# A two-layer SwiGLU and mixer trunk on eight cores: later due dates in two listings, joined sums, an end by halves

## The chip, the cores and the metric

One Trainium2 chip, eight cores. Every core runs the same program on one of the eight sequences of the batch (2048 tokens, 1024 channels), so nothing is exchanged between cores. The metric is the device time of the slowest core, in microseconds (us). Engines: TensorE (PE; PEld is its weight load), VectorE (DVE), ScalarE (ACT), GpSimd (POOL), SyncE (SP), and 16 DMA engines per core.

## The reference

Two layers, each three sub-layers; every one is x += gate * f(RMSNorm(x) * (1 + scale) + shift), with gate, scale and shift from the conditioning vector.

```python
for l in range(2):
    mod = silu(c) @ w_mod[l] + b_mod[l]                    # 9 x 1024 values for the sequence
    h, gate = modulate(x, norm_g[l, 0], mod_f1)
    x = x + 0.5 * gate * swiglu(h, w_ffn_in[l, 0], w_ffn_out[l, 0])   # 1024 -> 2 x 2816 -> 1024
    h, gate = modulate(x, norm_g[l, 1], mod_mx)
    if l == 0: y = mixer_ab(h, ...)      # projections to 2560, layernorm + chunk mixing of "v", short conv, projection
    else:      y = mixer_pool(h, ...)    # trailing-window means (2, 4, 8, 16), 256 x 256 per group
    x = x + gate * y
    h, gate = modulate(x, norm_g[l, 2], mod_f2)
    x = x + 0.5 * gate * swiglu(h, w_ffn_in[l, 1], w_ffn_out[l, 1])
return rmsnorm(x, final_g)
```

## The kernel before

**Tiling.** Channels lie on the partitions, tokens in tiles of 512 columns (`TT`). X holds the whole stream in f32 (4 token tiles x 8 chunks of 128 channels). A phase is one sub-layer for one pair of token tiles (p = 0: tiles 0 and 1, p = 1: tiles 2 and 3), ten phases in all; the pooling mixer runs in the background of phases of the second layer.

**Seven products for eight.** A pair of token tiles, a pair of halves of the contraction and a pair of output blocks form a 2 x 2 block product, computed with seven block products instead of eight (`class Unit`, P1 to P7). That needs sums of blocks ahead of TensorE, in f16 on VectorE: of the weights in `piece_sums` (a piece of 128 x 2048 lands in a slot; four dependent 128x512 operations make four more blocks), of h in `h_sums`, of the activations g*u in `a_sums`, called when a gate-up unit is done. There are also sums on the results: P6 and P7 each have a `tensor_tensor` on PSUM (rows `ps<-ps,TP` and `TP<-ps,TP`), and ScalarE copies two PSUM banks per unit. An FFN phase has two groups (m = 5 and 6 blocks per half); each group is gate-up units (28 matmuls each), then four down units (7 m matmuls each), u = 0 to 3, each for two output chunks. `LastUnit` does the same in eight plain products, without sums; before it is used in two groups (`PLAIN`) and for the last down unit of the program.

**Order.** Python code calls `add` for every instruction; `Timeline` gives each a planned start. TensorE's order is that in which the code calls the products: `segments` interleaves unit v's rest with unit u's start (u1 u5 v7 v3 u2 v4 u6, and v4 before u2 where a down unit u follows a gate-up unit v). At the end `relist` (once) sets VectorE's and ScalarE's order anew: of what is ready, the instruction with the earliest due date goes first. A due date is the smaller of what the users of the result need and the planned start plus 8 (`due.append`). `emit` writes one in-order queue per engine, with semaphore waits; all instructions have the line of `op.fn(E)` in `run`, L442 in the profile.

**Mixer of layer 0** (`ab_phase`): per 128 tokens a projection, Gelu, `bn_stats`, `bn_aggr`, two small POOL operations for 1/sqrt, and a `tensor_scalar` on VectorE for the normalised values; then four down units opened as u1 u5 w1 w5 u2 u6 ....

**Statistics.** `squares` makes x^2 on ScalarE and adds pairs on VectorE; `ones_mm` sums over partitions on TensorE. The code puts that matmul into TensorE's order 0.3 after the planned end of the sum, or at once where `bg_drain` empties the background work ahead of a group's down units.

**The end** (`end_phase`): down units 0, 1, 2 in seven products, unit 3 plain: its two chunks for tile 2, then its two for tile 3. Then squares, ones matmul, `rstd` (Ln, Exp on ScalarE), and `final_chunk` for 16 blocks of 128x512: x * g * rstd in one VectorE operation each, and a DMA out per two chunks.

## Time and profile before

| | |
|---|---|
| runs | 1965.75, 1962.3, 1962.87 us; median 1962.87 |
| the profiled execution | 1963.22 us; span of its slowest core 1961.7 us, of all cores 1947.1 to 1961.7 |
| PE / PEld / DVE / ACT / POOL busy | 96% / 44% / 89% / 52% / 9% of the span |
| mean granted TensorE clock | 0.979 to 0.993, by core |

The profiled execution is 1.5 us longer than its span and 0.35 us longer than the median. A matmul's record is longer than its pitch, since matmuls overlap: counts and waits tell more than busy time. "[x <-DVE ...]" behind a row is the time its engine sat idle before it, and who ended that.

### The profile page before, as it was taken

Reading aid. Unit: us, or ns where it says so; the run is one execution under the profiler, and the core shown is the slowest. Engines: PE = TensorE matmul, PEld = TensorE weight load, DVE = VectorE, ACT = ScalarE, POOL = GpSimd, SP = SyncE. Lnnn points to the kernel's source line nnn. Section 1 sums busy time; section 2 is a strip of 40 time slices with the busy share of each in tenths; the row PEclk is TensorE's granted clock in tenths of the full one; section 3 lists DMA queues with packets and bytes.
Section 4 is the critical chain, followed back from the end, with each engine's and each line's share of the span. In section 5 each row is a group of like instructions: output and inputs, shape, how many; then the busy total and the mean of one; then the engine's idle time right before and its main releaser. Section 6 shows DMA issues by size and latency. Waiting matters only on the chain.

```text
span 1961.7 us, 25716 instructions; the slowest of 8 cores (1947.1 to 1961.7 us)
## 1 busy us (share of the span) xinstructions
PE 1883.8 (96%) x8656; PEld 854.2 (44%) x8656; DVE 1749.7 (89%) x3788; ACT 1011.1 (52%) x1692; POOL 172.5 (9%) x330
## 2 busy tenths in 40 slices
PE   6999999999999899999999999999999999899996
PEld 5444444444434344444444444444443444344442
DVE  3989999989998999999999988986999779998985
ACT  4545565455363564465446544655457535664343
...
GB/s 285 163 193 193 157 100 166 167 95 173 192 108 160 107 122 161 182 111 148 153 180 118 129 81 93 83 91 96 75 76 65 97 75 81 59 96 89 165 85 104
DMA packets 67519, 248.73 MB, mean 127 GB/s; under 512 B 7616, under 2 KB 7744, under 8 KB 67136
## 3 DMA queue, kind: packets, MB, share of 16 engines
...
q14 instruction: 54, 0.44, 0.1%
...
## 4 chain that ended last, share of the span: by engine, by line
PE 79%; DVE 11%; DMA 9%; issue 1%; SPq 0%; ACT 0%; POOL 0%; DVEq 0%; POOLq 0%; ACTq 0%
PE ps L442 79%; DVE TP L442 3%; DMA SLOTS<-wout 2%; DMA SLOTS<-win 2%; DVE ACTB L442 2%; DMA ACTB<-wmod 2%; DVE X L442 2%; DVE SLOTS L442 1%; DMA SLOTS<-wab 1%; DVE WMOD L442 1%; DVE ps L442 1%; DMA WMOD<-wmod 1%; DVE SQ L442 1%; SPq L442 0%; DVE H L442 0%
## 5 line engine op out<-in xcount | busy, mean ns | idle before, releaser
L442 PE MATMUL ps<-H,SLOTS 128*128 128x512 f16 x5440 | 1200.3, 379 | 10.4 <-DVE ps L442 4.4
L442 PEld LDWEIGHTS ps<-H,SLOTS 128*128 128x128 f16 x5440 | 530.3, 98 | 659.2 <-issue 29.6
L442 ACT ACTIVATE ps<-ps 128x512 f32<-128x512 f32 x654 | 379.9, 582 | 522.9 <-PE ps L442 490.6
L442 PE MATMUL ps<-ACTB,SLOTS 128*128 128x512 f16 x2716 | 612.6, 382 | 22.1 <-DVE ACTB L442 9.6
L442 DVE TENSOR_TENSOR SLOTS<-SLOTS 128x512 f16<-128x512 f16 x1044 | 415.3, 417 | 27.2 <-DMA SLOTS<-win 14.0
L442 PEld LDWEIGHTS ps<-ACTB,SLOTS 128*128 128x128 f16 x2716 | 263.6, 98 | 358.6 <-issue 55.0
L442 ACT ACTIVATE TP<-ps 128x512 f32<-128x512 f32 x463 | 275.8, 596 | 166.5 <-PE ps L442 164.0
L442 DVE TENSOR_TENSOR ACTB<-TP,ps 128x512 f16<-128x512 f32 x368 | 249.3, 683 | 31.0 <-PE ps L442 18.2
L442 DVE TENSOR_TENSOR TP<-ps,TP 128x512 f32<-128x512 f32 x239 | 164.3, 687 | 68.8 <-ACT ps L442 67.4
L442 ACT ACTIVATE SQ<-X 128x512 bf16<-128x512 f32 x224 | 133.9, 623 | 144.8 <-DVE X L442 102.0
L442 DVE SCALAR_TENSOR_TENSOR X<-ps,GH,X 128x512 f32<-128x512 f32 x257 | 189.5, 745 | 16.2 <-PE ps L442 15.1
L442 POOL DMA_DIRECT2D SLOTS<-win x176 | 93.1, 529 | 1036.5 <-PE ps L442 981.3
L442 DVE SCALAR_TENSOR_TENSOR WMOD<-WMOD,CB 128x512 f32<-128x512 f32 (+1 forms) x258 | 175.7, 688 | 5.6 <-DMA WMOD<-wmod 5.5
L442 DVE TENSOR_TENSOR ps<-ps,TP 128x512 f32<-128x512 f32 x239 | 166.2, 695 | 15.6 <-PE ps L442 11.6
L442 ACT ACTIVATE H<-TP,MODT,AS 128x512 f16<-128x512 f32 x160 | 123.2, 805 | 33.6 <-DVE TP L442 20.2
L442 DVE TENSOR_TENSOR ACTB<-ACTB 128x512 f16<-128x512 f16 x338 | 136.5, 419 | 0.9
L442 DVE TENSOR_TENSOR TP<-X,RS 128x512 f32<-128x512 f32 x192 | 127.5, 683 | 1.2 <-ACT RS L442 0.9
L442 POOL DMA_DIRECT2D SLOTS<-wout x88 | 46.5, 528 | 541.3 <-PE ps L442 541.3
L442 DVE TENSOR_TENSOR SQ<-SQ 128x1024 bf16<-128x1024 bf16 (+1 forms) x104 | 55.6, 541 | 2.3 <-ACT SQ L442 2.2
L442 PE MATMUL ps<-SQ,ONES 128*128 128x512 bf16 x82 | 32.4, 449 | 21.2 <-DVE SQ L442 12.0
L442 DVE SCALAR_TENSOR_TENSOR X<-TP,GH,X 128x512 f32<-128x512 f32 x63 | 46.8, 742 | 0.0
L442 DVE TENSOR_TENSOR H<-H 128x1024 f16<-128x1024 f16 (+1 forms) x72 | 43.4, 623 | 0.1
...
## 6 DMA issues: line engine op xcount, KB each, us to landing
...
ACTB<-wmod SPq DMA_DIRECT2D x10, 512.0 KB, 24.7
...
```

The source lines that it names most:

```text
L442: return lambda E: getattr(E, name)(*a, **k)
```

## The change

- `relist` runs twice, and the planned start plus 40 takes the place of plus 8.
- Joined sums: in `piece_sums` two of four operations become one with a 128x2x512 output, whose first input is a block read twice; the blocks are stored in another order for it (`W11` ... `S4`). `h_sums` and `a_sums` get `two_sums` in the same way, and `a_sums` for m > 4 handles two blocks at a time where it can.
- FFN down units open with two units in step (`run_down`, `ORDER_DOWN`); the other order strings say what the code did before.
- The end: one down unit in seven products (was three), units 1, 2 and 3 plain; all of tile 2 first, then tile 3 in two halves of 256 tokens. The gain g is multiplied in on ScalarE, 1/rms on VectorE for two chunks at once, and stored per half.
- The mixer's normalised values: `activation` on ScalarE with two more small POOL operations for its bias, instead of `tensor_scalar` on VectorE. In the pooling mixer the copy of one column (`SLAST`) goes to ScalarE (24 copies become 18).
- The ones matmul is placed 2.5 (was 0.3) after the sum's planned end.

```diff
+SLACK_DUE = 40.0
-            due.append(o.start + (0.0 if o.eng == "pe" else 8.0))
+            due.append(o.start + (0.0 if o.eng == "pe" else SLACK_DUE))
...
+    W11, W12, W22, W21, S1, S2, S4 = 2, 3, 1, 4, 0, 5, 6
...
-                if (l, i, p, g) not in PLAIN and not (last and g == len(GROUPS) - 1 and 4 * x >= 3 * m):
+                if (l, i, p, g) not in PLAIN and not (last and g == len(GROUPS) - 1 and 4 * x >= m):
...
-        tt_(v(4), v(3), v(2), ALU.add, [k(2), k(3)], [k(4)], n=w, half=True)
-        tt_(v(3), v(0), v(3), ALU.subtract, [k(0), k(3)], [k(3)], n=w, half=True)
-        tt_(v(5), v(4), v(0), ALU.subtract, [k(4), k(0)], [k(5)], n=w, half=True)
-        tt_(v(6), v(1), v(5), ALU.subtract, [k(1), k(5)], [k(6)], n=w, half=True)
+        both = SL[:, s, :].rearrange("p (q k) -> p q k", k=512)
+        add("dve", I("tensor_tensor", out=both[:, S1:W21 + 1:W21 - S1, 0:w], in0=v(W21).unsqueeze(1).broadcast_to([128, 2, w]),
+                     in1=both[:, W22:W11 + 1:W11 - W22, 0:w], op=ALU.subtract), reads=[k(W22), k(W11), k(W21)],
+            writes=[k(S1), k(W21)], cost=c_dve(2 * w, True))
+        tt_(v(S2), v(W11), v(S1), ALU.subtract, [k(W11), k(S1)], [k(S2)], n=w, half=True)
+        tt_(v(S4), v(W12), v(S2), ALU.subtract, [k(W12), k(S2)], [k(S4)], n=w, half=True)
...
-        return [q] if h == 2 else list(range(q, q + h)), op.end + 0.3
+        return [q] if h == 2 else list(range(q, q + h)), op.end + 2.5
...
+    def two_sums(view, at, n, k):
+
+        add("dve", I("tensor_tensor", out=view[:, 1:6:4, at:at + n], in0=view[:, 3, at:at + n].unsqueeze(1).broadcast_to([128, 2, n]),
+                     in1=view[:, 1:5:3, at:at + n], op=ALU.add), reads=k(1) + k(3) + k(4), writes=k(1) + k(5), cost=c_dve(2 * n, True))
...
     def a_sums(m, i, half, apart=False):
         w = 1
+        if not apart and m > 4 and i < m - 2 + m % 2:
+            if i % 2 == 0:
+                return
+            w = 2
+        i += 1 - w
...
+    ORDER_DOWN = "u1 u5 v7 v3 v4 w1 u2 u6 w5 w2 u7 u3 w6 u4"
+    ORDER_AB = "u1 u5 w1 w5 u2 u6 u7 u3 w2 u4 w6"
...
-            ts(Av4[:, blk, :], TP[:, gv, 0:TT], STAT[:, st, 6:7], STAT[:, st, 9:10], ALU.subtract, ALU.mult,
-               [("TP", gv), ("ST", st)], [("A", blk)], n=TT)
+            add("pool", I("tensor_tensor", out=STAT[:, st, 8:9], in0=STAT[:, st, 6:7], in1=STAT[:, st, 9:10], op=ALU.mult),
+                reads=[("ST", st)], writes=[("ST", st)], cost=0.3)
+            add("pool", I("tensor_scalar", out=STAT[:, st, 7:8], in0=STAT[:, st, 8:9], scalar1=-1.0, scalar2=None, op0=ALU.mult),
+                reads=[("ST", st)], writes=[("ST", st)], cost=0.3)
+            act(Av4[:, blk, :], TP[:, gv, 0:TT], AF.Identity, [("TP", gv), ("ST", st)], [("A", blk)], src="sb",
+                scale=STAT[:, st, 9:10], bias=STAT[:, st, 7:8])
...
-                        add("dve", I("tensor_copy", SLAST[:, ch:ch + 1], PMS[:, (tt + 1) * TT - 1:(tt + 1) * TT]), reads=[("PMS", tt)],
-                            writes=[("SLAST", ch)], cost=0.07)
+                        if p == 0 or tt == 0:
+                            act(SLAST[:, ch:ch + 1], PMS[:, (tt + 1) * TT - 1:(tt + 1) * TT], AF.Copy, [("PMS", tt)], [("SLAST", ch)], n=1,
+                                src="sb")
...
+    def run_down(units, side):
+
+        v = pend.pop()
+        a, b = units[:2]
+        for n, f in enumerate(in_order(ORDER_DOWN, u=a, w=b, v=v)):
+            f()
...
+        def scaled(t, c, rk, keys, base=(), lo=0, w=TT):
+
+            out = X[:, t, c:c + 2, lo:lo + w]
+            ok = ("OUT", t, c + 1) if w == TT else ("OUT", t, c + 1, lo)
+            add("dve", I("tensor_tensor", out=out, in0=out, in1=RS[:, t % 2, lo:lo + w].unsqueeze(1).broadcast_to([128, 2, w]), op=ALU.mult),
+                reads=keys + list(base) + rk, writes=keys, cost=c_dve(2 * w))
...
+        pair(0, 0, TT)
+        for lo in (0, W):
+            for u in units:
+                for dd in range(2):
+                    b = bank(hold=True)
+                    u.part(dd, 1, 0, n, b, lo, W)
+                    held.discard(b)
+                    if (u, dd, lo) == (a, 1, 0):
+                        tile2()
+                    flush_halves()
...
-                    run_units([DownUnit(l, s, p, os_, m, u, final) for u in range(3 if final else 4)], side)
+                    units = [DownUnit(l, s, p, os_, m, u, final) for u in range(1 if final else 4)]
+                    (run_units if final else run_down)(units, side)
...
-    Sd.relist()
+    for _ in range(2):
+        Sd.relist()
```

**What the change moves.** TensorE, the opening of the first group of down units in the program, before (banks are numbered; `H,SLOTS` are gate-up products of unit v, `ACTB,SLOTS` down products, five matmuls each):

```order
L442 MATMUL ps5<-ACTB,SLOTS 128x512 x5
L442 MATMUL ps4<-ACTB,SLOTS 128x512 x5
L442 MATMUL ps0<-H,SLOTS 128x512 x4
L442 MATMUL ps1<-H,SLOTS 128x512 x4
L442 MATMUL ps2<-H,SLOTS 128x512 x4
L442 MATMUL ps5<-ACTB,SLOTS 128x512 x5
L442 MATMUL ps3<-ACTB,SLOTS 128x512 x5
L442 MATMUL ps0<-ACTB,SLOTS 128x512 x5
L442 MATMUL ps2<-ACTB,SLOTS 128x512 x5
L442 MATMUL ps3<-ACTB,SLOTS 128x512 x5
```

And with the change:

```order
L445 MATMUL ps4<-ACTB,SLOTS 128x512 x5
L445 MATMUL ps5<-ACTB,SLOTS 128x512 x5
L445 MATMUL ps0<-H,SLOTS 128x512 x4
L445 MATMUL ps1<-H,SLOTS 128x512 x4
L445 MATMUL ps2<-H,SLOTS 128x512 x4
L445 MATMUL ps5<-ACTB,SLOTS 128x512 x5
L445 MATMUL ps4<-ACTB,SLOTS 128x512 x5
L445 MATMUL ps3<-ACTB,SLOTS 128x512 x5
L445 MATMUL ps2<-ACTB,SLOTS 128x512 x5
L445 MATMUL ps5<-ACTB,SLOTS 128x512 x5
```

Before, u2 (the second product into ps5) follows v4 (ps2) at once. With the change, w1 (ps5, now the other unit's bank) stands between v4 and u2 (ps4).

VectorE at the end of the layer-0 mixer, p = 1, between two `ps<-ps,TP` sums that release P3 of the first and of the second down unit (`TP<-X,RS` and `H<-H` build the next phase's h), before:

```order
L442 SCALAR_TENSOR_TENSOR X<-ps,GH,X 128x512
L442 TENSOR_TENSOR TP<-X,RS 128x512 x2
L442 SCALAR_TENSOR_TENSOR X<-ps,GH,X 128x512
L442 TENSOR_TENSOR TP<-X,RS 128x512 x2
L442 TENSOR_TENSOR SLOTS<-SLOTS 128x512
L442 TENSOR_TENSOR H<-H 128x1024
L442 TENSOR_TENSOR SLOTS<-SLOTS 128x512
L442 SCALAR_TENSOR_TENSOR X<-TP,GH,X 128x512
L442 TENSOR_TENSOR H<-H 128x1024 x2
L442 TENSOR_TENSOR ps<-ps,TP 128x512
```

And with the change, from the first of those sums to the second:

```order
L445 TENSOR_TENSOR ps<-ps,TP 128x512
L445 TENSOR_TENSOR TP<-X,RS 128x512 x2
L445 TENSOR_TENSOR SLOTS<-SLOTS 128x2x512
L445 TENSOR_TENSOR TP<-X,RS 128x512
L445 TENSOR_TENSOR TP<-ps,TP 128x512
L445 SCALAR_TENSOR_TENSOR X<-ps,GH,X 128x512 x3
L445 TENSOR_TENSOR ps<-ps,TP 128x512
```

Before, 19 instructions lie between the two sums, sums of h among them (the last part is shown); with the change 8 do, none of them on H.

The last instructions of VectorE, before:

```order
L442 SCALAR_TENSOR_TENSOR X<-ps,GH,X 128x512
L442 TENSOR_TENSOR SQ<-SQ 128x512
L442 SCALAR_TENSOR_TENSOR X<-ps,GH,X 128x512 x2
L442 SCALAR_TENSOR_TENSOR X<-X,SM,RS 128x512 x2
L442 TENSOR_TENSOR SQ<-SQ 128x512
L442 SCALAR_TENSOR_TENSOR X<-X,SM,RS 128x512 x14
```

And with the change:

```order
L445 TENSOR_TENSOR X<-X,RS 128x1024
L445 TENSOR_TENSOR SQ<-SQ 128x256
L445 SCALAR_TENSOR_TENSOR X<-ps,GH,X 128x256 x3
L445 TENSOR_TENSOR SQ<-SQ 128x256
L445 TENSOR_TENSOR X<-X,RS 128x2x256 x2
L445 SCALAR_TENSOR_TENSOR X<-ps,GH,X 128x256
L445 TENSOR_TENSOR X<-X,RS 128x2x256 x6
```

Before, 14 operations on 128x512 stand behind the last sum of squares; with the change two of 2x256 stand ahead of the last projection's result, two and then the last four behind it.

Counts over the program: TensorE has 48 fewer 128x512 matmuls from ACTB and 12 fewer from WMOD (down products), and 144 new ones of 256 columns. VectorE goes from 3527 to 3039 instructions: 1040 `SLOTS` operations of 128x512 become 514 and 257 of 128x2x512; 338 on `ACTB` become 74, 52 of 1024, 28 of 2x512 and 26 of 2x1024; on `H` 56 of 1024 and 16 of 512 become 28, 14 of 2x1024, 8 of 512 and 4 of 2x512.

## Rows read from the trace of the kernel before

**Rows 1.** The page's first part: busy time by engine, share of the span, instructions.

```profile
PE 1883.8 (96%) x8656; PEld 854.2 (44%) x8656; DVE 1749.7 (89%) x3788; ACT 1011.1 (52%) x1692; POOL 172.5 (9%) x330
```

**Rows 2.** Stretches: length; busy us (instructions) per engine; TensorE clock; DMA share; GB/s.

```profile
60.00:1946.00 1886.00, 1840.82 (x8480) 821.88 (x8478) 1709.27 (x3680) 982.35 (x1648) 169.48 (x321) 1.00 0.61 121
640.00:700.00 60.00, 52.36 (x224) 21.82 (x222) 59.37 (x121) 37.88 (x63) 4.22 (x8) 0.94 0.48 94
1460.00:1482.00 22.00, 18.36 (x77) 7.63 (x76) 19.93 (x47) 12.62 (x24) 1.06 (x2) 0.92 0.41 70
```

**Rows 3.** TensorE's waits from 60 to 1946: total us, times, longest.

```profile
PE ps L442 <- DVE ps L442: 11.8, 15, 3.1
PE ps L442 <- DVE ACTB L442: 10.8, 16, 1.5
PE ps L442 <- DVE SQ L442: 9.4, 6, 2.1
```

**Rows 4.** Timeline, TensorE at openings of down groups: start, us, what, [idle before].

```profile
126.68 4.69 PE L442 MATMUL ps<-ACTB,SLOTS 128*128 128x512 f16 x21 [0.41 <-DVE ACTB L442]
...
1803.85 24.12 PE L442 MATMUL ps<-ACTB,SLOTS 128*128 128x512 f16 x111 [0.30 <-DVE ACTB L442]
```

**Rows 5.** Timeline, TensorE at the ends of the layer-0 mixer's two phases.

```profile
549.78 2.53 PE L442 MATMUL ps<-ACTB,SLOTS 128*128 128x512 f16 x11 [0.15 <-ACT CARRY L442]
...
670.70 10.27 PE L442 MATMUL ps<-ACTB,SLOTS 128*128 128x512 f16 x40 [3.15 <-DVE ps L442]
...
685.13 1.89 PE L442 MATMUL ps<-ACTB,SLOTS 128*128 128x512 f16 x8 [0.25 <-DVE ps L442]
```

**Rows 6.** Timeline, TensorE where statistics are forced in ahead of a down group.

```profile
1461.22 9.66 PE L442 MATMUL ps<-H,SLOTS 128*128 128x512 f16 x44
...
1473.46 0.38 PE L442 MATMUL ps<-SQ,ONES 128*128 128x512 bf16 x1 [2.14 <-DVE SQ L442]
...
1475.54 4.44 PE L442 MATMUL ps<-ACTB,SLOTS 128*128 128x512 f16 x12
...
1697.68 0.59 PE L442 MATMUL ps<-SQ,ONES 128*128 128x512 bf16 x1 [1.50 <-DVE SQ L442]
```

**Rows 7.** Groups by shape: count, busy us, mean ns of one, idle before.

```profile
L442 DVE TENSOR_TENSOR SLOTS<-SLOTS 128x512 f16<-128x512 f16 x1040 | 414.2, 418 | 27.2 <-DMA SLOTS<-win 14.0 <-DMA SLOTS<-wout 6.6 <-DMA SLOTS<-wab 3.5
L442 DVE TENSOR_TENSOR ACTB<-ACTB 128x512 f16<-128x512 f16 x338 | 136.5, 419 | 0.9
L442 DVE TENSOR_TENSOR H<-H 128x1024 f16<-128x1024 f16 x56 | 37.3, 682 | 0.0
L442 DVE SCALAR_TENSOR_TENSOR X<-X,SM,RS 128x512 f32<-128x512 f32 x32 | 22.5, 745 | 0.0
L442 DVE TENSOR_SCALAR ACTB<-TP,STAT 128x512 f16<-128x512 f32 x16 | 8.7, 541 | 3.3 <-POOL STAT L442 3.2
L442 DVE SCALAR_TENSOR_TENSOR WMOD<-WMOD,CB 128x1024 f32<-128x1024 f32 x2 | 2.5, 1226 | 2.4 <-DMA WMOD<-wmod 2.4
L442 DVE TENSOR_TENSOR TP<-X,RS 128x512 f32<-128x512 f32 x192 | 127.5, 683 | 1.2 <-ACT RS L442 0.9
```

**Rows 8.** Timeline, TensorE's matmuls of 128 columns.

```profile
501.67 1.06 PE L442 MATMUL ps<-WSM,ACTB 128*128 128x128 f16 x16
```

**Rows 9.** Timeline, the end.

```profile
1946.31 0.75 DVE L442 SCALAR_TENSOR_TENSOR X<-ps,GH,X 128x512 f32<-128x512 f32 x1 [2.27 <-PE ps L442]
...
1947.09 0.63 ACT L442 ACTIVATE SQ<-X 128x512 bf16<-128x512 f32 x1 [1.87 <-DVE X L442]
1948.30 0.42 DVE L442 TENSOR_TENSOR SQ<-SQ 128x512 bf16<-128x512 bf16 x1
...
1948.63 9.36 DVE L442 SCALAR_TENSOR_TENSOR X<-X,SM,RS 128x512 f32<-128x512 f32 x14
...
1949.27 0.69 ACT L442 ACTIVATE RS<-ps,GS 128x512 f32<-128x512 f32 x1 [1.55 <-PE ps L442]
1949.99 0.63 ACT L442 ACTIVATE RS<-RS 128x512 f32<-128x512 f32 x1
```

More of the change, by code:

```diff
@@ L670, in slk @@
     def slk(pc):
-        return [("SL", pc.slot, q) for q in range(4)]
+        return [("SL", pc.slot, q + pc.base // 512) for q in range(4)]
     def piece_sums(pc):
@@ L1109, in build_nc, with in_order @@
     pend = []
+    def in_order(text, **units):
+        at = dict(zip("1234567", range(7)))
+        return [(u.P1, u.P2, u.P3, u.P4, u.P5, u.P6, u.P7)[at[x[1]]] for x in text.split() for u in [units[x[0]]]]
+    ORDER_GG = "u1 u5 v7 v3 u2 v4 u6"
+    ORDER_DD = "u1 u5 v7 v3 u2 v4 u6"
+    ORDER_DG = "u1 u5 v7 v3 u2 v4 u6"
+    ORDER_DOWN = "u1 u5 v7 v3 v4 w1 u2 u6 w5 w2 u7 u3 w6 u4"
+    ORDER_AB = "u1 u5 w1 w5 u2 u6 u7 u3 w2 u4 w6"
     def segments(u, v):
@@ L1515, in run_units @@
             pend.append(u)
+    def run_down(units, side):
[3 more added lines that the diff above has]
+            f()
+            next(side, None)
+            if n >= 5:
+                while carry:
+                    carry.pop(0)()
+            pump()
+        pend.append(b)
+        run_units(units[2:], side)
     def run_plain(units, side):
@@ L1559, in down_side, with end_phase @@
             yield from build_h(nxt)
-    def end_phase(u):
+    def end_phase(units):
         sq = []
@@ L1574, in end_phase, with whole, sq_each @@
+        def whole(u, dd, tt):
+            b = bank(hold=True)
+            u.part(dd, tt, 0, n, b)
+            held.discard(b)
+        def sq_each(t):
+            out = []
+            for c in (6, 7):
+                z = sq_rot.next()
+                act(SQ[:, z, :], Xv(c, t), AF.Square, [Xk(c, t)], [("SQ", z)], src="sb")
+                out.append(z)
+            return out
         v = pend.pop()
+        v.P7()
+        v.P3()
         b = bank(hold=True)
-        v.P7()
-        for t in (2, 3):
-            for c in (0, 2):
-                sq_of(c, t)
@@ L1589, in end_phase, with tile2 @@
         flush_ones()
-        b = bank(hold=True)
-        sq_of(6, 2)
-        u.part(0, 1, 0, n, b)
-        held.discard(b)
-        sq_of(4, 3)
-        b = bank(hold=True)
-        flush_ones()
-        u.part(1, 1, 0, n, b)
-        held.discard(b)
-        sq_of(6, 3)
-        flush_ones(True)
-        rstd([2], True)
-        for c in range(NC):
-            final_chunk(2, c)
-        rstd([3], True)
-        for c in range(NC):
-            final_chunk(3, c)
+        W = TT // 2
+        def tile2():
+            flush_ones(True)
+            for z in last:
+                ones_mm(z, 2, 5)
+            rstd([2], True)
+            for c in range(NC):
+                gain(c, 2)
+            for c in range(0, NC, 2):
+                scaled(2, c, [("RS", 0)], [Xk(c, 2), Xk(c + 1, 2)])
@@ new lines, in end_phase, with square, pair @@
+        ones = []
+        count = {0: 0, W: 0}
+        def square(c, lo, w=W):
+            z = sq_rot.next()
+            act(SQ[:, z, lo:lo + w], X[:, 3, c, lo:lo + w], AF.Square, [Xk(c, 3)] + [Xk(c, 3) + (x,) for x in range(lo, lo + w, W)],
+                [("SQ", z)], n=w, src="sb")
+            return z
+        def pair(c, lo, w=W):
+            y, z = square(c, lo, w), square(c + 1, lo, w)
+            op = tt_(SQ[:, y, lo:lo + w], SQ[:, y, lo:lo + w], SQ[:, z, lo:lo + w], ALU.add, [("SQ", y), ("SQ", z)], [("SQ", y)],
+                     n=w, half=True)
+            ones.extend([(op.end + 0.3, y, x) for x in range(lo, lo + w, W)])
@@ new lines, in finish @@
+        def finish(lo):
+            keys = [("RS", 1, lo)]
+            for f, src, sk, kw in ((AF.Ln, PS[7], [("ps", 7)], dict(bias=EPSB, scale=1.0 / D)), (AF.Exp, RS[:, 1, :], keys, dict(scale=-0.5))):
+                add("act", I("activation", out=RS[:, 1, lo:lo + W], in_=src[:, lo:lo + W], func=f, **kw), reads=sk + ["EPSB", ("RS", 1)],
+                    writes=keys + ([("RS", 1)] if lo == 0 and f == AF.Ln else []), cost=0.5)
+            for c in range(0, NC, 2):
+                scaled(3, c, keys, [Xk(c + x, 3) + (lo,) for x in range(2)], [Xk(c, 3), Xk(c + 1, 3)], lo, W)
@@ new lines, in flush_halves @@
+        def flush_halves(every=False):
+            while ones and (every or ones[0][0] <= Sd.tl["pe"].tail()):
+                _, z, lo = ones.pop(0)
+                mm(PS[7][:, lo:lo + W], ONES[:], SQ[:, z, lo:lo + W], sum(count.values()) == 0, True, [("SQ", z), "ONES"], [("ps", 7)], n=W)
+                count[lo] += 1
+                if count[lo] == 5:
+                    finish(lo)
+        pair(0, 0, TT)
+        for lo in (0, W):
+            for u in units:
+                for dd in range(2):
+                    b = bank(hold=True)
+                    u.part(dd, 1, 0, n, b, lo, W)
+                    held.discard(b)
+                    if (u, dd, lo) == (a, 1, 0):
+                        tile2()
+                    flush_halves()
+                if u is e:
+                    op = [square(c, lo) for c in (6, 7)]
+                    ones.extend([(Sd.tl["act"].tail() + 0.3, z, lo) for z in op])
+                else:
+                    pair(2 * u.u, lo)
+                for c in ((0, 1) if u is a else ()) + (2 * u.u, 2 * u.u + 1):
+                    gain(c, 3, lo, W)
@@ L1680, in build_nc @@
         marks.append((sub, p, t_begin, Sd.tl["pe"].tail(), len(Sd.ops)))
-    add("sp", None, reads=[("OUT", t, c) for t in range(4) for c in (1, 3, 5, 7)], cost=0.01)
-    Sd.relist()
+    add("sp", None, reads=[("OUT", t, c) for t in range(3) for c in (1, 3, 5, 7)] + [("OUT", 3, c, lo) for c in (1, 3, 5, 7) for lo in (0, TT // 2)],
+        cost=0.01)
+    for _ in range(2):
+        Sd.relist()
     with nc.Block() as block:
```

90 lines of the change are left out of this document (51 added, 39 removed).

## The prediction

> **What bounds the kernel now.** I read the page first. TensorE is busy 96% of the span, VectorE 89%, ScalarE 52%, GpSimd 9% [rows 1]: TensorE sets the time, VectorE feeds it with little to spare. The stretches come next. From 60 to 1946 us TensorE's records cover 1840.8 of 1886, VectorE's 1709 [rows 2], so there are 45 us of idle TensorE in the body; in 640 to 700 VectorE is busy 59.4 of 60, and the clock is 0.94 there, 0.92 in 1460 to 1482 [rows 2]. TensorE's waits in the body then name the releaser: VectorE for a PSUM sum 11.8 us, for an activation block 10.8, for a sum of squares 9.4 [rows 3], 32.0 together in 37 waits; the rest of the 45 is smaller kinds. A wait costs more than its idle: 44 matmuls take 9.66 us [rows 6], a pitch of 0.216, while one record is 0.38, so each wait also shows 0.16 as busy that is not work (0.379 - 0.216).
>
> The timelines tell where they are. (a) Twelve waits at the openings of down groups, 0.22 to 1.00 us, 5.6 in sum (first and last in [rows 4]): TensorE sits in u2, whose last block comes from v4 just before. (b) Fourteen at the ends of the mixer's two phases, 11.9 in sum, the longest 3.15 (first, longest and last in [rows 5]). (c) Four waits, 7.3 in sum, for the last two sums of squares forced in ahead of a down group, at two places [rows 6]. (d) Past 1946 all is tail: the last projection's result is taken at 1946.31, and then VectorE works off 16 final operations until 1957.99 [rows 9], the last DMA lands at 1961.7; 15.4 us.
>
> **The change part by part.** The sum is against the profiled execution, 1963.2 us (span 1961.7), 0.3 above the median of the runs.
>
> *The end.* Its TensorE work grows: units 1 and 2 take 8 x 6 matmuls for 7 x 6, 12 more at 0.216 = 2.6 us. Half of tile 3's columns at a time means 144 matmuls of 256 columns in place of 72 of 512. Sixteen of 128 columns take 1.06 us [rows 8], (1.06 - 0.22)/15 = 0.056 each, so a weight load does not slow short matmuls here; 256 columns then cost half of 0.216, and halving costs nothing. The Trainium skill, page "TensorE: Matmul & The Clock Gate", section "Back-to-back issue gap", says the opposite: a stream of weight loads and matmuls is to be reckoned with 81 ns per matmul of 128 columns, not 56. By it each of the 144 would cost 25 ns more, 3.6 us in all, and the end would gain little; this case's 56 ns disagrees with it, and the sum goes by the row. The wait for a sum at 1930 (0.9, with restart 1.0) goes with the units that caused it. So the last projection is done 1.6 us later.
>
> What comes behind it, from the last result on: scale and add, 256 columns: 0.75 - 0.27 = 0.48. Square on ScalarE 0.63 - 0.21 = 0.42, with 0.03 ahead. From there through the ones matmul to the start of Ln: 0.44 (now 0.55, from the sum of squares' end at 1948.72 to 1949.27 [rows 9], less 0.11 for half the columns). Ln 0.48 and Exp 0.42 (0.69 and 0.63 in [rows 9], less 0.21 each). Four operations of 2x256 in f32: as one of 512, 0.68 [rows 7], pitch 0.60: 2.5. Then the DMA: 1957.99 to 1961.7 now, 3.7; halves are smaller, in shorter rows: I keep 3.6, bounds 3.0 and 4.8. Sum 8.4 for 15.4, a gain of 7.0. Net for the end: 7.0 - 1.6 = 5.4; I take 5.0, bounds 2.5 (the DMA long, VectorE behind with tile 2's rows) and 7.
>
> *VectorE's load.* A joined operation of 2x512 f16 is in no row. Bounds: 0.682, what a plain 128x1024 f16 takes [rows 7], and 1.226, a 128x1024 at one element per cycle (f32) [rows 7]. I take 0.68: type and inner rows of 512 are those of the nearest row, only the outer step differs. The Trainium skill, page "Vector Engine (DVE) Microarchitecture Reference", section "Performance modes — why throughput varies by op and dtype", says that a two-source 16-bit operation which reads one row again and again keeps two elements per cycle; no run shown here has it, and by it the price would also be 0.68. Sums by durations of [rows 7]: SLOTS 1040 x 0.418 = 434.7 becomes 257 x 0.68 + 514 x 0.418 = 389.6, -45.1. ACTB 338 x 0.419 = 141.6 becomes 74 x 0.419 + 80 x 0.68 + 26 x 1.21 = 116.9, -24.7. H -2.8. Normalised values 16 x 0.541, -8.7. SLAST, final work and fewer result sums about -6. Together -87, so VectorE falls from 1750 to some 1663 us, 5%. Alone it is worth nothing, since VectorE is not the bound; it counts where TensorE waits for it.
>
> *(a) Openings.* w1 is put between v4 and u2, five or six matmuls, 1.1 to 1.3 us, over waits of 0.2 to 1.0: they go. 5.6 + 12 x 0.16 = 7.5; I take 6.5, since u's pieces are released one product later and the joined activation sums come later for the block of an even index. Bounds 3 and 7.5.
>
> *(b) Mixer.* TensorE's order is the same; VectorE's is not. The 3.15 wait is for a PSUM sum behind 19 instructions; now it has 8 ahead, none on H. But VectorE is full in 640 to 700, and the h sums must still be done before the next phase's products: part of the wait moves there. At stake: 11.9 idle, 14 x 0.16 = 2.2 of restarts, 60 x 0.06 = 3.6 of clock. Of 17.7 I take 8.0, bounds 2 and 15.
>
> *(c) Squares.* They are done earlier: fewer VectorE instructions ahead. The 12 matmuls behind the wait take 4.44 instead of 2.75 [rows 6], the clock having fallen between its levels 2.4 and 1.2 GHz after TensorE idled. At stake 7.3 + 2 x 1.7 + 0.6 = 11.3; I take 7.0, bounds 2 and 11. The same later placing (2.5 for 0.3) helps the other two squares waits.
>
> *The rest.* 45 - 0.9 - 5.6 - 11.9 - 7.3 = 19.3 us of single waits, most behind VectorE. A fifth goes with its load: 3.5, bounds 0 and 10. New costs, named and not seen: VectorE's queue in pure order of need (far work may stand ahead of nothing, so a slip of a weight DMA stops more urgent work behind it), SLAST now through ScalarE between two scans, two more POOL operations ahead of weight DMAs in POOL's queue: +3, bounds 0 and 8.
>
> Sum: -5.0 - 6.5 - 8.0 - 7.0 - 3.5 + 3.0 = -27.0. 1963.2 - 27 = 1936.2, by the median 1935.9: 1936.
>
> **Rivals.** *The waits move.* VectorE is at 59.4 of 60 where it matters, order alone gives it no time, and a wait taken from one product comes back at the next phase's start. Then only the end and half of (a) are gained, 5 + 3.3, less the new costs of 3: 1958. For it: nearly full VectorE around the mixer. Against: (c) and (a) are waits beside a VectorE with 9% idle (1709 of 1886).
>
> *Nearly all goes.* If VectorE keeps pace everywhere, the body's 45 idle us go, 7.6 of restarts with them (some 48 waits) and 7 of clock, and 7 in the tail less 2.6: about 1900 to 1910; 1906. Against: the two DMA waits and the first microseconds are not touched.
>
> *Slower: the joined operations run at one element per cycle.* The place is every piece's sum, on VectorE. The joined ones are 289 of 2x512 and 40 of 2x1024, 369 times 1024 elements; at 1.226 they cost 0.54 more each, 201 us: VectorE would go to 1663 + 201 = 1864, 114 more than now. It decides at 87/369 = 0.24 over 0.68: above 0.92 for a 2x512 the load is higher than before. With 177 us idle in the body, but none around the mixer and at group changes, I reckon that half of 114 shows, less 15 of ordering and end: +42, 2005. For it: no row with such a pattern. Against: nothing in the type or the inner rows differs.
>
> **How the numbers follow.** What this kernel's measurement tells from no change is about 0.2%, 4 us. Forecast (1922 to 1950): 0.62. Waits move (1950 to 1962): 0.18. Nearly all goes (under 1922): 0.12. Joined operations slow, 0.04, and another slower way, say bunching by later due dates, 0.04. The range 1910 to 1960 takes in nearly all of the first two and half of the third. Faster by over 0.2% (below 1959): forecast, nearly all, and three quarters of the second: 0.87; within: 0.05; slower: 0.08.
>
> **What would show it.** In the profile after: `SLOTS` 2x512 at 0.68; VectorE near 1663 busy; no waits of 0.2 to 1.0 in u2 at openings; squares waits under 1 us at both places and no clock under 1.0 there; the mixer's longest wait under 1.5; the last 2x256 operation some 4.9 us after the last projection's result and the span's end 8.4 after it; 256-column matmuls 0.108 apart. Wrong if the waits of [rows 3] total over 30 us again, if a 2x512 takes over 0.92, or if the tail stays over 11 us.

## The result and the profile after

The changed kernel took 1940.56 us (median of 4 runs, 1938.63 to 1941.76) against 1962.59 for the kernel before in the same session: ratio 0.9873 [0.9828, 0.9918], 22.0 us less. The forecast was 1936 (1910 to 1960). In all that follows, executions in which a core's granted clock lay below 0.977 took 19 us or more longer, whatever the kernel, so times and differences are medians over the others, and only the ratios of the experiments contain some of them. In the profiled execution the slowest core's span fell from 1961.7 to 1938.7; the medians over the eight cores are 1953.6 and 1929.2.

The page's first part, after; it answers to [rows 1]:

```profile
PE 1882.2 (97%) x8747; PEld 865.3 (45%) x8747; DVE 1706.6 (88%) x3300; ACT 1035.3 (53%) x1752; POOL 185.5 (10%) x362
```

VectorE's busy time fell by 43 us (1749.7 to 1706.6), not by 87. (The page counts the reads of accumulators as instructions of their own, hence 3788 and 3300 for the program's 3527 and 3039.) Stretches of the kernel after (length, busy us and instructions per engine, TensorE clock, DMA share, GB/s), as in [rows 2]:

```profile
60.00:1925.00 1865.00, 1835.88 (x8526) 829.03 (x8525) 1671.04 (x3203) 1003.20 (x1699) 182.52 (x353) 1.00 0.62 123
640.00:700.00 60.00, 54.78 (x249) 23.68 (x248) 59.41 (x108) 40.97 (x67) 4.77 (x9) 1.00 0.51 103
540.00:575.00 35.00, 32.45 (x142) 14.00 (x141) 33.22 (x61) 22.23 (x37) 3.18 (x6) 0.95 0.52 107
1430.00:1480.00 50.00, 47.74 (x214) 21.02 (x212) 47.85 (x85) 32.98 (x61) 3.18 (x6) 0.97 0.44 74
```

In 640 to 700 TensorE now gets 249 matmuls in, 224 before, beside the same full VectorE (59.41 and 59.37). The clock is whole there; at the mixer's first end (540 to 575) it is 0.95, where it was 1.00 before.

TensorE's waits, 60 to 1925 (total us, times, longest), against [rows 3]:

```profile
PE ps L445 <- DVE ps L445: 8.2, 13, 1.5
PE ps L445 <- DMA SLOTS<-wab: 5.2, 4, 2.2
PE ps L445 <- DVE ACTB L445: 4.7, 5, 1.5
PE ps L445 <- DVE SQ L445: 4.6, 2, 2.3
PE ps L445 <- ACT ps L445: 3.5, 7, 1.3
```

The three kinds of [rows 3] went from 32.0 us in 37 waits to 17.5 in 20. The second line, waits for the mixer's weights, was 1.8 before, but it is no new cost: it differs from core to core (0 to 5.2 in this profile, 0 to 3.5 before), its mean over the eight cores is 1.5 for 1.6, and the slowest core is the one that had most of it. All waits between the first 60 us and the tail fell from 43.8 (53) to 28.4 (34) on the slowest core, from 36.3 to 22.6 in the mean of the eight.

The matmuls of a kind that occurs at fixed places of the program (the mixer's transposed products, the first matmul on `CB`) cut each core's span into the same stages in every kernel. Each stage's length is that between the starts of two such matmuls in the profiled execution; medians over the cores, us. The first two columns are the kernel before and the changed one in the session above; the others are from the experiments, whose batches ran on three chips (5, 7 and 4 on record). The column of the listing alone leaves out core 5; the kernel before took 1959.4, 1959.1 and 1958.5 on the three chips:

| stage | before | changed | changed, chip 5 | opening alone, chip 7 | listing alone, chip 4 | both, chip 4 |
|---|---|---|---|---|---|---|
| start | 51.9 | 52.4 | 52.0 | 51.6 | 51.8 | 51.1 |
| to the mixer | 412.6 | 412.6 | 408.6 | 411.5 | 413.0 | 411.5 |
| mixer p=0 to p=1 | 105.2 | 101.9 | 101.9 | 103.5 | 105.7 | 101.5 |
| to pooling p=0 | 802.8 | 798.2 | 798.0 | 799.3 | 802.7 | 795.6 |
| pooling p=0 to p=1 | 222.7 | 217.4 | 216.6 | 224.0 | 221.2 | 219.6 |
| in pooling p=1 | 72.9 | 72.1 | 72.1 | 72.9 | 72.1 | 72.2 |
| to the span's end | 284.6 | 275.8 | 275.8 | 286.3 | 282.2 | 281.7 |

The gain is 3.3 in the mixer, 4.6 behind it, 6.1 in the pooling and 8.8 in the last stage. The start, where TensorE waits for modulation weights, is what it was.

Groups by shape, after (busy us, mean ns of one, idle before), against [rows 7]; the joined operations are printed flat, 2x512 as 128x1024:

```profile
L445 DVE TENSOR_TENSOR SLOTS<-SLOTS 128x512 f16<-128x512 f16 x515 | 213.3, 417 | 3.2
L445 DVE TENSOR_TENSOR SLOTS<-SLOTS 128x1024 f16<-128x1024 f16 x257 | 175.4, 683 | 18.6 <-DMA SLOTS<-win 14.3 <-DMA SLOTS<-wout 4.0
```

TensorE at the mixer's two ends, after, against [rows 5]:

```profile
554.49 0.38 PE L445 MATMUL ps<-ACTB,SLOTS 128*128 128x512 f16 x1 [1.50 <-DVE ACTB L445]
555.76 18.25 PE L445 MATMUL ps<-ACTB,SLOTS 128*128 128x512 f16 x76 [0.90 <-DVE ps L445]
...
658.80 0.38 PE L445 MATMUL ps<-ACTB,SLOTS 128*128 128x512 f16 x1 [1.50 <-DVE ACTB L445]
660.08 16.56 PE L445 MATMUL ps<-ACTB,SLOTS 128*128 128x512 f16 x76 [0.91 <-DVE ps L445]
```

The wait of 3.15 at 670.70 has no counterpart any more: 76 matmuls run through from 660.08.

The end, VectorE, after (start, us, what, [idle before]); it answers to [rows 9]:

```profile
1929.61 1.29 DVE L445 TENSOR_TENSOR X<-X,RS 128x512 f32<-128x512 f32 x2
1930.81 0.48 DVE L445 SCALAR_TENSOR_TENSOR X<-ps,GH,X 128x256 f32<-128x256 f32 x1
1931.21 1.28 DVE L445 TENSOR_TENSOR X<-X,RS 128x512 f32<-128x512 f32 x2
1933.15 2.50 DVE L445 TENSOR_TENSOR X<-X,RS 128x512 f32<-128x512 f32 x4 [0.66 <-ACT RS L445]
```

The last of the final operations ends at 1935.65, 4.84 us after the last projection's result is taken at 1930.81 (forecast 4.9), and the span's end is 7.9 after it (forecast 8.4, before 15.4). VectorE even waits 0.66 for 1/rms: the two operations that stand ahead are done by then.

### The profile page after: what moved, and what is told of

Read it like the earlier page. It is cut to its first block, busy times and chain, and to the rows that moved or that the text cites. A ratio compares the mean times of both kernels' runs of the same rounds, so it can differ in the third digit from the quotient of the medians.

```text
span 1938.7 us, 25549 instructions; the slowest of 8 cores (1921.8 to 1938.7 us)
## 1 busy us (share of the span) xinstructions
PE 1882.2 (97%) x8747; PEld 865.3 (45%) x8747; DVE 1706.6 (88%) x3300; ACT 1035.3 (53%) x1752; POOL 185.5 (10%) x362
## 4 chain that ended last, share of the span: by engine, by line
PE 82%; DMA 9%; DVE 6%; ACT 1%; issue 1%; SPq 1%; POOL 1%; DVEq 0%; POOLq 0%
PE ps L445 82%; DMA SLOTS<-win 3%; DMA SLOTS<-wab 2%; DMA ACTB<-wmod 2%; DVE ACTB L445 1%; DMA WMOD<-wmod 1%; DVE TP L445 1%; DVE X L445 1%; DVE SLOTS L445 1%; DVE ps L445 1%; SPq L445 1%; DMA SLOTS<-wout 1%; POOL STAT L445 0%; DVE H L445 0%; DVE SQ L445 0%
## 5 line engine op out<-in xcount | busy, mean ns | idle before, releaser
L445 PE MATMUL ps<-H,SLOTS 128*128 128x512 f16 x5440 | 1202.3, 380 | 12.5 <-DVE ps L445 5.0
L445 PE MATMUL ps<-ACTB,SLOTS 128*128 128x512 f16 (+1 forms) x2812 | 612.1, 376 | 10.2 <-DVE ACTB L445 4.1
L445 PEld LDWEIGHTS ps<-ACTB,SLOTS 128*128 128x128 f16 x2812 | 275.1, 98 | 334.4 <-issue 24.9
L445 DVE TENSOR_TENSOR SLOTS<-SLOTS 128x512 f16<-128x512 f16 (+1 forms) x774 | 386.1, 505 | 21.8 <-DMA SLOTS<-win 14.3
L445 DVE TENSOR_TENSOR TP<-ps,TP 128x512 f32<-128x512 f32 x237 | 162.8, 687 | 72.9 <-ACT ps L445 71.7
L445 DVE SCALAR_TENSOR_TENSOR X<-ps,GH,X 128x512 f32<-128x512 f32 (+1 forms) x265 | 191.7, 732 | 26.3 <-PE ps L445 23.9
L445 ACT ACTIVATE SQ<-X 128x512 bf16<-128x512 f32 (+1 forms) x230 | 136.6, 613 | 142.3 <-DVE X L445 96.5
L445 DVE TENSOR_TENSOR ACTB<-ACTB 128x512 f16<-128x512 f16 (+2 forms) x180 | 117.3, 654 | 1.2
L445 DVE TENSOR_TENSOR SQ<-SQ 128x1024 bf16<-128x1024 bf16 (+2 forms) x104 | 54.2, 534 | 1.1 <-ACT SQ L445 0.7
L445 PE MATMUL ps<-SQ,ONES 128*128 128x512 bf16 (+1 forms) x89 | 34.0, 437 | 16.2 <-ACT SQ L445 6.6
L445 DVE TENSOR_TENSOR H<-H 128x1024 f16<-128x1024 f16 (+2 forms) x54 | 41.1, 782 | 0.9 <-ACT H L445 0.9
## 6 DMA issues: line engine op xcount, KB each, us to landing
X<-xT SPq DMA_DIRECT2D x2, 2048.0 KB, 21.2
```

Source lines behind the costliest of these rows:

```text
L445: return lambda E: getattr(E, name)(*a, **k)
```

## The experiments

They ran in three batches, each on a chip of its own and with the kernel before in it: the first four rows on chip 5, the next four on chip 7, the last four on chip 4. The time is a median over the number of executions behind it. The difference is to the kernel before in the same batch (1959.4 over 11 executions, 1959.1 over 14, 1958.5 over 3), with a 95% interval from resampling. The changed kernel ran in the first batch alone, so a row of the other two is set beside it by these differences.

| kernel | us (runs) | less than before | ratio, 95% |
|---|---|---|---|
| changed | 1935.2 (5) | 24.2 [22.8, 25.7] | 0.9826 [0.9761, 0.9891] |
| listing undone | 1949.3 (6) | 10.1 [8.7, 11.9] | 0.9983 [0.9929, 1.0037] |
| joined sums undone | 1938.3 (6) | 21.2 [19.3, 23.8] | 0.9841 [0.9782, 0.99] |
| opening undone | 1946.9 (5) | 12.5 [9.6, 14.8] | 0.9923 [0.9853, 0.9993] |
| end undone | 1941.5 (7) | 17.5 [15.4, 19.8] | 0.9898 [0.9847, 0.9949] |
| due 8, two passes | 1937.4 (5) | 21.7 [18.6, 24.3] | 0.9845 [0.9784, 0.9907] |
| due 40, one pass | 1935.3 (3) | 23.8 [22.1, 24.9] | 0.9864 [0.9782, 0.9946] |
| before + opening | 1956.1 (6) | 3.0 [0.9, 4.4] | 1.0002 [0.9949, 1.0055] |
| before + listing | 1951.0 (2) | 7.5 [5.0, 8.9] | 0.9972 [0.9906, 1.0038] |
| before + both | 1942.4 (2) | 16.2 [14.2, 17.0] | 0.9816 [0.9707, 0.9924] |
| values on VectorE | 1938.2 (4) | 20.3 [16.7, 21.5] | 0.9821 [0.9741, 0.99] |
| squares spread | 1929.7 (3) | 28.8 [25.7, 31.2] | 0.9812 [0.9726, 0.9898] |

**The changed kernel itself.** No edit.

> The changed kernel itself, as the yardstick beside the three that undo a part. By the result already seen it takes 1936 to 1944 us; both theories expect 0.987 of the kernel before.

24.2 less than before, 2 more than in the session of the result. The waits for the mixer's weights are 0 to 3.6 here, by core, 1.2 in the mean.

**The listing undone.**

```diff
-SLACK_DUE = 40.0
+SLACK_DUE = 8.0
-    for _ in range(2):
+    for _ in range(1):
         Sd.relist()
```

> The changed kernel with one listing and due dates of plus 8 again. Theory (order and load each take a share of the waits): 8 us more than the whole change, the waits of the mixer's end and for the sums of squares come back in part. Rival (the lighter VectorE does it, order is indifferent): within 2 us of the whole change. Second rival (order is nearly all of it): 15 us more.

14 us slower than the changed kernel, the most of any part. Its TensorE waits (total, times, longest) show part of where: the sums of squares are four waits again (2.00 and 1.16, 1.99 and 1.49 at the two places), and waits for a weight piece's sums have come:

```profile
PE ps L445 <- DVE SQ L445: 6.6, 4, 2.0
PE ps L445 <- DVE SLOTS L445: 4.6, 4, 1.8
```

**The joined sums undone.** The two operations for each joined one again, on the new order of blocks.

```diff
-        add("dve", I("tensor_tensor", out=both[:, S1:W21 + 1:W21 - S1, 0:w], ...
+        tt_(v(S1), v(W21), v(W22), ALU.subtract, [k(W22), k(W21)], [k(S1)], n=w, half=True)
+        tt_(v(W21), v(W21), v(W11), ALU.subtract, [k(W11), k(W21)], [k(W21)], n=w, half=True)
```

> The changed kernel with all joined sums split up again (weights, h, activations), in its own new order. VectorE gets 66 us more of work. Theory: 6 us more than the whole change. Rival (VectorE's load does not matter at 88% busy, only the order of its queue): within 2 us. Second rival (VectorE bounds the stretches around the mixer and the group changes): 15 to 20 us more.

3.1 us [0.3, 4.9]: between theory and first rival, and not told apart from the rival's 2. VectorE's busy time, 60 to 1900, the changed kernel on this chip first, then without joins:

```profile
60.00:1900.00 1840.00, 1812.22 (x8387) 815.37 (x8386) 1660.13 (x3184) 989.18 (x1671) 181.62 (x353) 1.00 0.61 124
```

```profile
60.00:1900.00 1840.00, 1808.61 (x8331) 811.74 (x8354) 1676.22 (x3607) 982.70 (x1662) 183.64 (x353) 1.00 0.62 124
```

423 more instructions cost 16 us of VectorE, 38 ns each. VectorE's timeline in the changed kernel shows most of the reason:

```profile
1455.62 0.68 DVE L445 TENSOR_TENSOR ACTB<-ACTB 128x1024 f16<-128x1024 f16 x1
1456.22 0.68 DVE L445 TENSOR_TENSOR SLOTS<-SLOTS 128x1024 f16<-128x1024 f16 x1
1456.82 0.42 DVE L445 TENSOR_TENSOR ACTB<-ACTB 128x512 f16<-128x512 f16 x1
1457.16 0.42 DVE L445 TENSOR_TENSOR SLOTS<-SLOTS 128x512 f16<-128x512 f16 x1
```

A record of 0.42 is followed by the next after 0.34, one of 0.68 after 0.60: the records overlap by 0.08. By these pitches (start to start) a piece costs 0.60 + 2 x 0.335 = 1.27 for 4 x 0.335 = 1.34, 0.07 less. The overlap is lost where an instruction waits for the one right ahead of it: it then starts 0.45 after a 128x512 and 0.72 after a joined one, and with joins that happens behind 92 of 772 `SLOTS` operations, without them behind 28 of 1028. The means over all unbroken pairs are 0.624 and 0.359 in the changed kernel, 0.345 without joins: 1.342 for 1.380, 0.038 a piece, which is the 38 ns.

**The opening undone.**

```diff
-                    (run_units if final else run_down)(units, side)
+                    run_units(units, side)
```

> The changed kernel with the down groups opened as before (second product right behind the last gate-up product). Theory: the twelve waits of 0.2 to 1.0 us per core come back, 6 us more than the whole change. Rival (they shrink by themselves with a lighter VectorE): 2 us more.

11.7 us slower, twice the theory. Its waits for an activation block:

```profile
PE ps L445 <- DVE ACTB L445: 13.9, 21, 2.6
```

More than the 10.8 in 16 of [rows 3], but only half of it stands at the openings: 6.9 in 17 waits there, for 5.6 in 12. The longest, 2.6, is ahead of a gate-up product at 378.95, and one of 2.5, ended by an operation on `TP`, has come at 796.57. All waits of the body, mean of the cores, are 31.8 (45) for the changed kernel's 22.4 (26): with 0.16 for each restart that makes 12.4, near the 11.7.

**The end undone.** `end_phase`, the 48 + 12 summed products and the final operations of before.

```diff
-units = [DownUnit(l, s, p, os_, m, u, final) for u in range(1 if final else 4)]
+units = [DownUnit(l, s, p, os_, m, u, final) for u in range(3 if final else 4)]
```

> The changed kernel with the end phase of before (three paired units and one last unit, tile 3 finished in whole tiles) and nothing else undone. Before ran at about 1959.4 us and the changed kernel at 1935.2 in the batch ahead of this. Theory (the prediction's term, 5.0): about 1940, with the last of the final operations some 12 us after the last projection's result and the span's end 15 us after it. Rival, the term was too small: the two traces show tails of 15.4 and 7.9, a difference of 7.5, which counts nearly in full because the 12 more matmuls (2.6) run under VectorE's work that had to be waited for anyway: 1942 or more. Second rival: the tail only moves work, VectorE being behind either way: under 1937.

6.7 us slower by the differences to before, nearer the first rival (interval of the 6.7: 4.3 to 9.7); the last stage alone is 4.3 longer (280.1 for 275.8). Its last rows on VectorE:

```profile
1921.52 0.75 DVE L445 SCALAR_TENSOR_TENSOR X<-ps,GH,X 128x512 f32<-128x512 f32 x1 [2.06 <-PE ps L445]
1922.97 0.43 DVE L445 TENSOR_TENSOR SQ<-SQ 128x512 bf16<-128x512 bf16 x1 [0.70 <-ACT SQ L445]
1923.49 10.69 DVE L445 SCALAR_TENSOR_TENSOR X<-X,SM,RS 128x512 f32<-128x512 f32 x16
```

The tail is 16.4 us again (1921.52 to 1937.9), 8.5 more than the new one, and the 12 matmuls fewer give 2.6 of it back: 5.9.

**Which half of the listing.** First the due date alone undone, then the second pass.

```diff
-SLACK_DUE = 40.0
+SLACK_DUE = 8.0
```

> The changed kernel with due dates 8 us after the instruction's own start again, but with the two listing passes kept. With both undone it ran at 1949.3, 14 over the changed kernel's 1935.2. Theory: the due date is what matters (with 8 us a far piece's sums are put ahead of an urgent sum of squares or of a PSUM sum), so most of the 14 shows: 1944 to 1950, and the waits for sums of squares are again four, 6 us together. Rival: the second pass does the work, since it lists from times that the first has made true: 1935 to 1939 here.

```diff
-    for _ in range(2):
+    for _ in range(1):
         Sd.relist()
```

> The changed kernel with due dates 40 us after, but with one listing pass instead of two. Theory (the due date is what matters): 1935 to 1940, two waits for sums of squares as in the changed kernel. Rival (the second pass matters): 1944 or more. If this and the kernel with 8 us and two passes are both near 1949, only the two together do it.

My theory that the due date alone matters fell: with 8 us and two passes the kernel is only 2.5 us worse [-0.3, 6.3], with 40 and one pass 0.4 [-1.2, 3.0]; neither can be told from nothing. The waits for sums of squares are two in both, not four. Both undone cost 14. Either edit does nearly all of the work by itself; together they are one gain and not two. Why either is enough, no run shows.

**The opening alone, on the kernel before.** `run_down` and its order, nothing else.

```diff
-                    run_units([DownUnit(l, s, p, os_, m, u, final) for u in range(3 if final else 4)], side)
+                    (run_units if final else run_down)([DownUnit(l, s, p, os_, m, u, final) for u in range(3 if final else 4)], side)
```

> The kernel before with the new opening of the output projections (two units in step, w1 between v4 and u2) and nothing else. Theory (the prediction's step a, 6.5, which the undoing put at 11.7): 6 to 12 less than before, about 1950, the waits of 0.2 to 1.0 in u2 gone from the trace. Rival (interaction): the new opening only pays where VectorE's order and load are the new ones; with due dates of 8 us and separate sums the waits move to w5 and u6: 1956 to 1960.

The rival held: 3.0, not 6 to 12. The waits for activation blocks are down as they should be, but TensorE waits elsewhere for VectorE:

```profile
PE ps L442 <- DVE ps L442: 10.3, 11, 3.3
PE ps L442 <- DVE SQ L442: 8.8, 7, 2.1
PE ps L442 <- DVE ACTB L442: 4.2, 6, 1.3
PE ps L442 <- DVE SLOTS L442: 3.5, 3, 1.3
```

By stages (table above, whose column of before is from another session) it gains 5.2 around the mixer and gives back 1.3 in the pooling and 1.7 at the end.

**The listing alone, and both, on the kernel before.**

```diff
-            due.append(o.start + (0.0 if o.eng == "pe" else 8.0))
+            due.append(o.start + (0.0 if o.eng == "pe" else 40.0))
-    Sd.relist()
+    for _ in range(2):
+        Sd.relist()
```

> The kernel before with the new listing alone: due dates 40 us after, two passes. Undone from the changed kernel the listing cost 14 us (1949.3 for 1935.2), the new opening 12; added to the kernel before, the opening gave 3.0 (1956.05 for 1959.07), since seven new waits for squares and PSUM sums stood where the twelve openings had been. Theory (the two need each other: both act on the same order of VectorE's queue, and either alone leaves the other's waits): the listing alone gives 2 to 6, 1953 to 1957. Rival (the parts add, and only the opening was weak on the old order): 10 to 14, 1945 to 1949.

> The kernel before with the new listing and the new opening, and neither the joined sums, nor the new end, nor the mixer's values on ScalarE. The whole change gave 24.2 on this chip, the end 6.4 when undone, the joined sums 3.1. Theory (the two need each other): 12 to 17 less than before, 1942 to 1947, more than the 3.0 of the opening and what the listing alone gives put together. Rival (they do not need each other, but each needs VectorE's lower load from the joined sums): 5 to 9, 1950 to 1954.

The listing alone gives 7.5, a little over the theory's 6 and under the rival's 10. Both give 16.2: 5.7 more than 3.0 + 7.5, as the theory of need said, though from two executions each. The cores' medians (52 and 28 spans) say it too: 9.4 for the listing, 18.7 for both, 4.1 for the opening. (The 24.2 and 3.1 that the expectation puts on this chip were measured on chip 5, the 6.4 for the end on chip 7.) In the stages, the pooling and the end, where the opening alone lost, gain 3.1 and 2.9 with both.

**The mixer's values and `SLAST` back on VectorE.**

```diff
+            ts(Av4[:, blk, :], TP[:, gv, 0:TT], STAT[:, st, 6:7], STAT[:, st, 9:10], ALU.subtract, ALU.mult,
+               [("TP", gv), ("ST", st)], [("A", blk)], n=TT)
```

> The changed kernel with the mixer's normalised values and the scans' last columns back on VectorE, nothing else undone. Theory: 16 operations of 0.541 and some 40 of 0.07 to 0.2 come back in the two mixer phases, where VectorE is at 59 of 60; a quarter to a half of these 9 to 12 us shows: +2 to +5 over the changed kernel's 1935.2 (24.2 under before). Rival: TensorE's waits in the mixer are for sums that stand ahead of these values in the queue, and nothing shows: within 1. Second rival: what ScalarE got stood in the way of its own PSUM copies, so undoing it gains: -1 to -3.

3.9 us slower than the changed kernel by the differences to before (20.3 for 24.2), in the theory's range; the interval [16.7, 21.5] does not reach 22.8. The normalised values and `SLAST` were not run apart.

**The squares spread.** The remaining waits of the changed kernel at the two pooling places read so on ScalarE, VectorE and TensorE, one after the other:

```profile
1460.93 1.15 ACT L445 ACTIVATE SQ<-X 128x512 bf16<-128x512 f32 x2 [1.34 <-PE ps L445]
```

```profile
1461.60 1.96 DVE L445 TENSOR_TENSOR SQ<-SQ 128x1024 bf16<-128x1024 bf16 x4
```

```profile
1460.52 0.59 PE L445 MATMUL ps<-SQ,ONES 128*128 128x512 bf16 x2
1463.37 0.90 PE L445 MATMUL ps<-SQ,ONES 128*128 128x512 bf16 x2 [2.26 <-DVE SQ L445]
1464.06 4.29 PE L445 MATMUL ps<-ACTB,SLOTS 128*128 128x512 f16 x12
```

ScalarE's last two squares start when the first of TensorE's ones matmuls has read its sum (1460.52 + 0.38 = 1460.90), after 1.34 us idle: the eight `SQ` buffers are two sets of four, and the last squares need the set that this matmul frees. Then VectorE sums, and TensorE, whose queue is in order, waits 2.26. A shorter queue on VectorE can't remove that: its four sums follow each other without anything between them. In the kernel before, at the same place, both causes are there. ScalarE's last three squares wait for the first ones matmul too, and among VectorE's sums stand three other instructions, 0.33 + 0.33 + 0.59 = 1.25 us by their pitches:

```profile
1471.14 1.67 ACT L442 ACTIVATE SQ<-X 128x512 bf16<-128x512 f32 x3 [0.31 <-PE ps L442]
```

```profile
1471.96 0.68 DVE L442 TENSOR_TENSOR SQ<-SQ 128x1024 bf16<-128x1024 bf16 x1
1472.56 0.42 DVE L442 TENSOR_TENSOR SLOTS<-SLOTS 128x512 f16<-128x512 f16 x1
1472.89 0.42 DVE L442 TENSOR_TENSOR SQ<-SQ 128x512 bf16<-128x512 bf16 x1
1473.23 0.42 DVE L442 TENSOR_TENSOR SLOTS<-SLOTS 128x512 f16<-128x512 f16 x1
1473.56 0.68 DVE L442 TENSOR_TENSOR SQ<-SQ 128x1024 bf16<-128x1024 bf16 x1
1474.17 0.68 DVE L442 TENSOR_TENSOR ACTB<-TP,ps 128x512 f16<-128x512 f32 x1
1474.76 0.42 DVE L442 TENSOR_TENSOR SQ<-SQ 128x512 bf16<-128x512 bf16 x1
```

These three are what the change took away: two waits of 3.64 in sum became one of 2.26. It is the new listing that does it. With the listing alone, and the ones matmul at its old place, each of the two places shows one wait, of 2.38; with the listing undone, and the ones matmul at its new place, each shows two again.

The next kernel removes the buffer wait. It puts one ones matmul behind each of u1, u5, v7 and v3 of the next group, and w2 ahead of u6, w6 ahead of u7 in `ORDER_AB`:

```diff
-                if last or not late_norm:
+                late = last and pm is not None
+                if not late and (last or not late_norm):
                     bg_drain()
...
             f()
+            if late and bg and n in (0, 1, 2, 3):
+                bg_step()
+            if late and n == 4:
+                bg_drain()
...
-    ORDER_AB = "u1 u5 w1 w5 u2 u6 u7 u3 w2 u4 w6"
+    ORDER_AB = "u1 u5 w1 w5 u2 w2 u6 w6 u7 u3 u4"
```

> The changed kernel with two more edits, at the places where its trace still waits. Where the mixer's chunks follow each other in pairs, w2 comes ahead of u6 and w6 ahead of u7; and at the two last groups before a mixer phase's end the four ones matmuls are put one after each of u1, u5, v7, v3 of the next output projection, not all four ahead of it. Theory: the two waits of 2.3 for sums of squares and the half clock behind them go (2 x 3), and 1.5 of the mixer's first waits: 4 to 7 less than the changed kernel, so 28 to 31 under before. Rival: the statistics are now late for the next normalisation, and the wait shows as one for H or ACTB: within 2 of the changed kernel, or slower.

28.8 under before: 4.6 [1.0, 7.4] better than the changed kernel, as the theory had it, and the fastest kernel of the study; cores' median 1922.0 for 1926.4. TensorE at the same place (core 0):

```profile
1453.64 0.38 PE L445 MATMUL ps<-SQ,ONES 128*128 128x512 bf16 x1
1453.86 1.03 PE L445 MATMUL ps<-H,SLOTS 128*128 128x512 f16 x4
1455.25 0.38 PE L445 MATMUL ps<-SQ,ONES 128*128 128x512 bf16 x1 [0.37 <-DVE SQ L445]
...
1457.12 0.38 PE L445 MATMUL ps<-SQ,ONES 128*128 128x512 bf16 x1 [0.63 <-DVE SQ L445]
...
1458.20 17.00 PE L445 MATMUL ps<-ACTB,SLOTS 128*128 128x512 f16 x78
```

Two waits of 0.37 and 0.63 in place of one of 2.26, and the 78 matmuls behind run at 0.216, the full rate ((17.00 - 0.38)/77). At the second place the waits are 0.47 and 0.30, and on all eight cores both places are alike. More `SQ` buffers, the other way out, were not tried, and the two edits were not run apart. They act in different stages, though: from mixer to mixer the cores' median is 99.5 for 101.9 (w2 and w6), in the two stages that hold the squares 215.1 for 216.6 and 272.7 for 275.8, all against the changed kernel on chip 5.

## Why the prediction was right, and which steps were not

The mechanism held in the main: VectorE's order and the tail set the time. The likeliest case (1922 to 1950) came, 4.6 us above its centre. That the sum came so near is in part luck: two steps of the body were put too high, and one, the single waits, too low. The terms below are read from the two slowest cores, 1963.2 us and 1940.2.

- **The end, 5.0.** 4.3 by the last stage, 6.7 by the time of the kernel without it; by the trace 15.4 - 7.9 - 2.6 = 4.9. The chain behind the last result was forecast at 8.4 and took 7.9. The wait at 1930 that was to go is still there (1893.24, 0.88): the matmuls on `WMOD` still open behind a PSUM sum.
- **Halved matmuls at nothing.** 84 of 256 columns take 9.33 us, (9.33 - 0.27)/83 = 0.109 each, half of 0.216 and 0.001:

```profile
1916.58 9.33 PE L445 MATMUL ps<-ACTB,SLOTS 128*128 128x256 f16 x84
```

  By the prediction's estimate from the 81 ns for 128 columns of the Trainium skill, page "TensorE: Matmul & The Clock Gate", section "Back-to-back issue gap", the end would have lost 3.6 more; this row does not bear it out.
- **(a) Openings, 6.5.** Of the twelve waits, two of 0.57 are left, at the plain groups that `run_down` does not open otherwise; 4.5 idle and ten restarts of 0.16 went, 6.1. Right by the trace, but no property of the edit: 3.0 alone, 11.7 when undone. The price of an order depends on what VectorE has queued at that moment.
- **(b) Mixer, 8.0.** Nine waits, 8.7 us, for fourteen, 11.9. With 5 restarts (0.8), the clock's 3.6 in 640 to 700 and 0.05 of 35 us lost at the first end (1.8), the gain is 5.8. The 3.15 wait is gone; the longest is 1.50, at both ends, with 0.90 behind it, where it was 1.47 and 1.25: this pair was untouched. "Part of the wait moves to the next phase" came as well (1.14 for `H`).
- **(c) Squares, 7.0.** This step failed. It said that the sums are late because VectorE has much ahead, and had the waits under 1 us; they are 2.26 and 2.31. VectorE's other work was 1.25 of 3.64, and went; the rest is the cycle through the `SQ` buffers, which the prediction did not have. From the first ones matmul to the down products it takes 3.54 us for 4.82 at the first place and 3.46 for 4.99 at the second. The clock, which was to be whole there, was not: the twelve matmuls behind take 4.29 and 4.44, before 4.44 and 4.15. The gain is 2.7. Over all cores the clock fell at 11 of the 16 places, before at all 16. The two other squares waits, 0.51 and 1.64, are gone, as forecast; they count in the rest.
- **The rest, 3.5.** The single waits, without those for the mixer's weights, fell from 16.4 us to 7.9: 8.5, more than twice the term. No run took them apart.
- **VectorE's load, -87.** The price of a joined operation was right: 0.683 for 1024 elements, where a plain 128x1024 takes 0.682. The Trainium skill, page "Vector Engine (DVE) Microarchitecture Reference", section "Performance modes — why throughput varies by op and dtype", states that a two-source operation which reads a row again and again keeps the mode with two results per cycle; the trace agrees. The sum was mis-sized: it took durations of records that overlap by 0.08. By the mean pitches of the two traces SLOTS save 23 and not 45 (1040 x 0.354 for 257 x 0.624 + 515 x 0.358), ACTB 10 and not 25. What the load was worth was put small, and is: 3.1.
- **New costs, +3.** None of those named is seen. The waits for the mixer's weights are 3.4 more between the two slowest cores, and the clock fell behind one of them (at 528.5, 1.7 us); over the eight cores they are not more than before.

Terms of the body by the trace: 6.1 + 5.8 + 2.7 = 14.6, for 21.5 forecast; (c) is over half of that miss. With 4.9 for the end and 8.5 for the rest, less 3.4 and 1.7, the two traces' terms come to 22.9; the executions differ by 23.0. Of the rivals, "the waits move" was seen in part (mixer, opening alone), and the joined operations do not run at one element per cycle.
